# A stack of two transformer blocks on one core: the moving rows of the weight matmuls are read by turns from their two halves

## The chip, the cores and the metric

One NeuronCore of a Trainium2 chip runs the whole program. The metric is device time in microseconds (us) of one execution, lower is better. The core has a matrix engine (TensorE, PE in the profile), VectorE (DVE), ScalarE (ACT), GpSimd (POOL) and SyncE (SP, which only issues DMAs here). They run side by side and meet at semaphores. SBUF is the working memory (128 partitions), PSUM the memory into which TensorE accumulates, in eight banks of 512 f32 columns a partition.

## The reference, cut to what matters

256 rows of 1024 values (`x`) go through two stacks, each of two layers. Nearly all the work is products of these 256 rows with f32 weight matrices:

```python
def first_block(x, ...):
    for layer in range(2):
        h = h + _mixer(rmsnorm(h), w_in[layer], w_ret_o, w_sb_o, w_out)   # 1024 x 6656 weights, then 3 smaller ones
        h = h + (silu(hn @ Wg) * (hn @ Wu)) @ w_down                      # FF = 2816
    return rmsnorm(h)

def second_block(x, mem, ...):
    for layer in range(2):
        x = x + 0.5 * swiglu(rms_norm(x), ffn1_w_in, ffn1_w_out)
        x = x + mixer(rms_norm(x))            # attention kinds, even or odd layer
        x = x + memory_cross_attention(rms_norm(x), rms_norm(mem), w_q, w_kv, w_o)
        x = x + 0.5 * swiglu(rms_norm(x), ffn2_w_in, ffn2_w_out)
```

Between the big products stand small ones (retention, stick-breaking, forgetting, differential, banded and cross attention over at most 256 positions).

## The kernel before, in words

The 256 rows are two tiles of 128 (`T = 2`). An activation is turned (transposed) by TensorE, scaled, and kept as two fp32r tiles: a rounded value `hi` and the rest `lo`. A weight matrix is cut into units of 1024 columns a partition: two rows of 512 weights (`kk` = 0, 1) out of two blocks of 128 of the contraction. Each unit is loaded by a DMA into one of four buffers `RAW`, ScalarE rounds it into `WH` (L1066), and VectorE writes the rest `RAW - WH` into `WL` (L1287); `WH` and `WL` have five buffers each.

For each unit, row `kk` and tile `t`, TensorE runs three matmuls into the same PSUM bank: `hi*WH` (L785), `hi*WL` (L786), `lo*WH` (L787). The activation is the stationary operand (128x128, loaded by a weight load, PEld in the profile), and the row of 512 weights is the moving operand, which streams from SBUF. A "chunk" is a product with 512 output columns: over a contraction of 1024 it has 8 blocks x 2 tiles x 3 = 48 such matmuls, into a pair of banks (one for each `t`), and the pairs `M0, M1` and `M2, M3` take turns. When a chunk is done, ScalarE or VectorE empties both its banks: copies with a scale (L1071, L1074, L1080, L1099), SiLU of the gate columns 0..255 (L1095) and the product with the up columns 256..511 (L1350), the residual add (L1345), the merge of two branches (L1475, L1479). The small products and the transposes use four other banks, `AUX`.

The order of everything is fixed beforehand: `Plan` gives each step a due time, and each engine runs its steps sorted by it (`for_pe`, `for_act`, `for_dve`). The change does not touch the plan.

Of the kernel before, what the change touches and what calls it, by code (L numbers as in the profile page):

```python
# [11 lines left out]
ACT = mybir.ActivationFunctionType  # L12
# [145 lines left out]
class Tmp:  # L158
    def __init__(self, first):
        self.first, self.final, self.i = first, first, None  # L160


BANKED = ("turn", "tq", "ret_s", "ret_o", "st_z", "st_s", "st_o", "cu1", "cu2", "df_s", "pt", "df_o", "hg_s", "hg_o",
# [596 lines left out]
def tensor(e, k):  # L760
    p = k.p
# [3 lines left out]
    for s in p.for_pe:  # L765
# [3 lines left out]
        if s.kind == "mm":  # L769
            c = s.c  # L770
            h = s.u % NHL
# [8 lines left out]
            if s.at0 and c.use[s.t] > 1:  # L780
                e.wait_ge(k.m_out[c.banks[s.t]], c.use[s.t] - 1)
            out = p.M[c.banks[s.t]][:, 0:s.ncol]
            wh = p.WH[:, h, s.kk * s.ncol:(s.kk + 1) * s.ncol]
            wl = p.WL[:, h, s.kk * s.ncol:(s.kk + 1) * s.ncol]
            e.matmul(out, s.hi, wh, start=s.at0, stop=False)  # L785
            e.matmul(out, s.hi, wl, start=False, stop=False)  # L786
            i = e.matmul(out, s.lo, wh, start=False, stop=s.final)  # L787
            if s.unit_end:
                i.then_inc(k.w_used, 1)
        elif s.kind == "narrow":  # L790
            c = s.c
            h = s.u % NHL
# [3 lines left out]
            out = p.M[c.banks[0]][0:s.ncol, 0:256]  # L796
            for kt in range(s.nk):
                wh, wl = (x[:, h, kt * s.ncol:(kt + 1) * s.ncol] for x in (p.WH, p.WL))
# [3 lines left out]
                i = e.matmul(out, wh, xl, start=False, stop=kt == s.nk - 1)  # L802
# [26 lines left out]
        elif s.kind == "tq":  # L829
# [9 lines left out]
            x = p.TMP[s.x.i]  # L839
# [22 lines left out]
        elif s.kind == "ret_o":  # L862
            x = p.TMP[s.x.i]
# [8 lines left out]
        elif s.kind == "st_z":  # L872
# [6 lines left out]
            if s.mate is not None:  # L879
                z, x = s.mate, p.AUX[s.mate.bank]  # L880
# [18 lines left out]
        elif s.kind == "st_o":  # L899
# [13 lines left out]
            for x, v, out in zip(xs, s.v, outs):  # L913
                i = e.matmul(out[:, 128:256], v[:, 1, :], x[:, 128:256], start=False, stop=True)
            i.then_inc(k.aux_full[b], 1)
        elif s.kind == "cu1":
# [3 lines left out]
            x = p.TMP[s.x.i]  # L920
# [122 lines left out]
def scalar(e, k):  # L1043
# [5 lines left out]
    for s in p.for_act:  # L1049
# [3 lines left out]
        if s.kind in ("rope", "vals", "plainx", "ff", "hq", "rg"):  # L1053
            c = s.c
            e.wait_ge(k.w_used, c.done)
            if s.norm.n > r_have:
                r_have = s.norm.n
                e.wait_ge(k.r_made, r_have)
            banks = [p.M[x] for x in c.banks]
            r = [s.norm.r[:, t:t + 1] for t in range(T)]  # L1060
        if s.kind == "conv":
            i, h = s.u % NRAW, s.u % NHL
# [4 lines left out]
        elif s.kind in ("rope", "plainx"):  # L1067
            if s.kind == "rope" and s.n == 3:
                e.wait_ge(k.d_tabx, 16)
            for t in range(T):  # L1070
                e.activation(p.TMP[s.xs[t].i], banks[t][:, :], ACT.Copy, scale=r[t]).then_inc(k.m_out[c.banks[t]], 1)  # L1071
        elif s.kind == "vals":
            for t in range(T):
                e.activation(s.dst[t], banks[t][:, :], ACT.Copy, scale=r[t]).then_inc(k.m_out[c.banks[t]], 1)  # L1074
        elif s.kind == "gate":
            c = s.c
            e.wait_ge(k.w_used, c.done)
            e.wait_ge(k.rh_made, s.rh.n)
            for t in range(T):
                e.activation(s.dst[t], p.M[c.banks[t]][:, :], ACT.Copy, scale=s.rh.out[:, t:t + 1]).then_inc(k.m_out[c.banks[t]], 1)  # L1080
        elif s.kind == "rg":
            table = "s"
            for t in range(T):
                e.activation(s.silu[t], banks[t][:, :], ACT.Silu, scale=r[t]).then_inc(k.m_out[c.banks[t]], 1)
        elif s.kind == "tanh":
            table = "s"
            for q in s.gates:
# [4 lines left out]
        elif s.kind == "ff":  # L1092
            table = "s"
            for t in range(T):
                e.activation(s.silu[t], banks[t][:, 0:256], ACT.Silu, scale=r[t]).then_inc(k.silu_made, 1)  # L1095
        elif s.kind == "hq":
            for t in range(T):
                x = p.TMP[s.xs[t].i]
                e.activation(x, banks[t][:, :], ACT.Copy, scale=r[t]).then_inc(k.m_out[c.banks[t]], 1)  # L1099
                e.wait_ge(k.m_out[c.banks[t]], c.use[t])  # L1100
                if s.n > 1:
                    e.wait_ge(k.hq_sum, 2 * (s.n - 2) + t + 1)
                e.activation(p.AS[:, 2 * t:2 * t + 2, :].rearrange("p a c -> p (a c)"), x, ACT.Square).then_inc(k.hq_sq, 1)
# [161 lines left out]
def vector(e, k):  # L1265
# [4 lines left out]
    for s in p.for_dve:  # L1270
# [3 lines left out]
        if s.kind in ("ff", "ch", "res", "mer1", "mer2"):  # L1274
            c = s.c
            e.wait_ge(k.w_used, c.done)
            banks = [p.M[x] for x in c.banks]
        if s.kind in ("ff", "ch", "rh", "fin", "cu1"):
            if s.norm.n > r_have:
                r_have = s.norm.n  # L1280
# [40 lines left out]
        elif s.kind in ("st_o", "hg_o"):  # L1321
            e.wait_ge(k.hi_made, s.hi_n)
            e.tensor_tensor(s.lo, aux[:, 0:256], s.hi.bitcast(F32), ALU.subtract).then_inc(k.aux_out[b], 1)
        elif s.kind == "cx_o":
            e.wait_ge(k.hi_made, s.hi_n)
            e.tensor_tensor(s.lo, aux[:, :], s.hi.bitcast(F32), ALU.subtract).then_inc(k.aux_out[b], 1)
        elif s.kind == "gains":
            e.wait_ge(k.aux_out[b], s.use)
            if s.n == 3:
                for i in range(2):  # L1330
                    e.tensor_scalar(p.GT[:, 144 + i:145 + i], p.GT[:, 136 + 2 * i:137 + 2 * i], 0.125, None, ALU.mult)
                for i in range(4):
                    l, j = i // 2, i % 2
                    q = e.tensor_scalar(p.GT[:, 146 + i:147 + i], p.GT[:, 128 + 4 * l + j:129 + 4 * l + j], 0.0625, None, ALU.mult)
                q.then_inc(k.su_gain, 1)
        elif s.kind == "norm":
            e.wait_ge(k.sq_sum, 2 * s.sq.n)
            e.tensor_tensor(s.a, s.ss[:, 0:4:2], s.ss[:, 1:4:2], ALU.add).then_inc(k.dve_chain, 1)
            chain += 1
            e.wait_ge(k.dve_chain, chain)  # L1340
            e.tensor_scalar(s.v, s.a, 1.0 / D, EPS, ALU.mult, ALU.add).then_inc(k.ms_made, 1)
        elif s.kind == "res":
            for t in range(T):
                x = p.X[:, t, s.half * 512:(s.half + 1) * 512]
                e.scalar_tensor_tensor(out=x, in0=banks[t][:, :], scalar=s.scale, in1=x, op0=ALU.mult,  # L1345
                                       op1=ALU.add).then_inc(k.m_out[c.banks[t]], 1)
        elif s.kind == "ff":
            for t in range(T):
                e.wait_ge(k.silu_made, 2 * (s.n - 1) + t + 1)
                e.scalar_tensor_tensor(out=s.h[t], in0=banks[t][:, 256:512], scalar=r[t], in1=s.silu[t], op0=ALU.mult,  # L1350
                                       op1=ALU.mult).then_inc(k.m_out[c.banks[t]], 1)
        elif s.kind == "ret_s":
            if s.n == 1:
                e.wait_ge(k.d_dec, 16)
            e.wait_ge(k.aux_full[b], s.use)
            e.tensor_tensor(p.TMP[s.x.i][:, 0:384], aux[:, 0:384], p.DEC[:, s.h, :], ALU.mult).then_inc(k.aux_out[b], 1)
        elif s.kind == "ret_o":
            e.wait_ge(k.aux_out[b], s.use)
            e.bn_stats(s.st[:, 0:6], s.dst[:, 0, :])
            e.bn_stats(s.st[:, 6:12], s.dst[:, 1, :]).then_inc(k.dve_chain, 1)  # L1360
            chain += 1
            e.wait_ge(k.dve_chain, chain)
            e.bn_aggr(s.mv[:, 0:2], s.st[:, 0:6])
            e.bn_aggr(s.mv[:, 2:4], s.st[:, 6:12]).then_inc(k.dve_chain, 1)
            chain += 1
        elif s.kind == "ret_v":
            e.wait_ge(k.dve_chain, chain)
            e.tensor_scalar(s.v, s.mv[:, 1:16:2], 1.0, EPS, ALU.mult, ALU.add).then_inc(k.var_made, 1)
        elif s.kind in ("ret_n", "hn", "bo_n") and s.first_use:
            q = s.rs  # L1370
            e.wait_ge(k.rs_guess, q.n)
            e.tensor_tensor(q.a, q.y, q.y, ALU.mult).then_inc(k.dve_chain, 1)
            chain += 1
            e.wait_ge(k.dve_chain, chain)
            e.scalar_tensor_tensor(out=q.c, in0=q.a, scalar=-0.5, in1=q.v, op0=ALU.mult, op1=ALU.mult).then_inc(k.dve_chain, 1)
            chain += 1
            e.wait_ge(k.dve_chain, chain)
            e.scalar_tensor_tensor(out=q.out, in0=q.c, scalar=1.5, in1=q.y, op0=ALU.add, op1=ALU.mult).then_inc(k.dve_chain, 1)
            chain += 1
            e.wait_ge(k.dve_chain, chain)  # L1380
# [91 lines left out]
        elif s.kind == "mer1":  # L1472
            e.wait_ge(k.tanh_made, s.tanh.n)
            for t in range(T):
                e.scalar_tensor_tensor(out=p.TMP[s.xs[t].i], in0=s.g[t], scalar=1.0, in1=banks[t][:, :], op0=ALU.add,  # L1475
                                       op1=ALU.mult).then_inc(k.m_out[c.banks[t]], 1)
        elif s.kind == "mer2":
            for t in range(T):
                e.scalar_tensor_tensor(out=s.g[t], in0=s.g[t], scalar=1.0, in1=banks[t][:, :], op0=ALU.add,  # L1479
                                       op1=ALU.mult).then_inc(k.m_out[c.banks[t]], 1)  # L1480
            for t in range(T):
                x = p.TMP[s.xs[t].i]
# [64 lines left out]
            e.tensor_scalar(x[:, cut:end], x[:, cut:end], q.rc[:, 1:2], None, ALU.mult).then_inc(k.probs, 1)  # L1547
        elif s.kind == "ch":
            for t in range(T):
                x = p.TMP[s.xs[t].i]  # L1550
                e.wait_ge(k.m_out[s.cc.c.banks[t]], s.cc.c.use[t])
                e.scalar_tensor_tensor(out=x, in0=banks[t][:, :], scalar=r[t], in1=x, op0=ALU.mult, op1=ALU.mult).then_inc(k.m_out[c.banks[t]], 1)
        elif s.kind == "cv":
            if s.n == 1:
                e.wait_ge(k.zeroed, 2)
# [350 lines left out]
```

## Time and profile before

| what | us |
|---|---|
| median of 3 runs (lowest, highest) | 2069.71 (2069.34, 2070.16) |
| the profiled execution | 2067.88 |
| its span, first to last instruction | 2065.7 |
| TensorE busy | 2042.6 |
| VectorE busy | 1234.0 |
| ScalarE busy | 1111.7 |

Busy time says for how much of the span an engine had an instruction in it. Matmuls overlap in the pipeline, so the duration of one (0.39 us) is not what it costs: that is the distance from one start to the next, which the timeline and the chain show. The profiled execution lies 1.8 us below the median of the runs.

### The profile page before, as it was taken

Reading aid. Unit: us, or ns where it says so; the run is one execution under the profiler, and the core shown is the slowest. Engines: PE = TensorE matmul, PEld = TensorE weight load, DVE = VectorE, ACT = ScalarE, POOL = GpSimd, SP = SyncE. Lnnn points to the kernel's source line nnn. Section 1 sums busy time; section 2 is a strip of 40 time slices with the busy share of each in tenths; the row PEclk is TensorE's granted clock in tenths of the full one; section 3 lists DMA queues with packets and bytes.
Section 4 is the critical chain, followed back from the end, with each engine's and each line's share of the span. In section 5 each row is a group of like instructions: output and inputs, shape, how many; then the busy total and the mean of one; then the engine's idle time right before and its main releaser. Section 6 shows DMA issues by size and latency. Waiting matters only on the chain.

```text
span 2065.7 us, 25169 instructions
## 1 busy us (share of the span) xinstructions
PE 2042.6 (99%) x9627; PEld 1674.2 (81%) x9627; DVE 1234.0 (60%) x1721; ACT 1111.7 (54%) x1682; POOL 36.3 (2%) x60
## 2 busy tenths in 40 slices
PE   8999999999999999999999999999999999999999
PEld 7878888888778888888887888888888888788887
DVE  6576665565766655655567765655555566655553
ACT  6575544455755544644457665544444465655442
POOL 0000100000000000000000000000000000000000
PEclk9999999999999999999999999999999999999999
DMA  7545566555456665566554344565565553545653
GB/s 251 163 143 174 179 186 185 189 177 160 153 172 193 188 190 188 180 190 187 187 167 142 120 157 152 179 187 185 183 184 187 190 185 131 173 143 163 184 184 132
DMA packets 258214, 359.76 MB, mean 174 GB/s; under 512 B 16908, under 2 KB 152288, under 8 KB 258096
## 3 DMA queue, kind: packets, MB, share of 16 engines
q1 hardware_dynamic: 256016, 352.75, 54.2%
q0 software_dynamic: 2080, 5.41, 0.9%
q8 instruction: 77, 1.26, 0.2%
q14 instruction: 41, 0.34, 0.0%
HBM read 357.04 MB, written 1.06 MB: 173 GB/s over the span
## 4 chain that ended last, share of the span: by engine, by line
PE 94%; DVE 3%; ACT 2%; issue 1%; POOL 0%; DMA 0%; SPq 0%; DVEq 0%; ACTq 0%
PE M L785 28%; PE M L787 28%; PE M L786 28%; PE AUX L827 3%; DVE WL L1287 1%; PE AUX L841 1%; PE AUX L1039 1%; PE AUX L1017 1%; ACT WH L1066 1%; PE AUX L963 1%; PE AUX L978 0%; PE AUX L969 0%; DVE RET L1470 0%; DVE SM L1436 0%; PE AUX L1004 0%
## 5 line engine op out<-in xcount | busy, mean ns | idle before, releaser
L1287 DVE TENSOR_TENSOR WL<-RAW,WH 128x1024 fp32r<-128x1024 f32 x669 | 815.9, 1222 | 650.2 <-ACT WH L1066 647.4
L1066 ACT ACTIVATE WH<-RAW 128x1024 fp32r<-128x1024 f32 x669 | 706.5, 1058 | 660.6 <-PE M L787 654.5
L785 PE MATMUL M<-WH,Bh 128*128 128x512 f32 x1792 | 718.8, 401 | 2.3 <-DVE WL L1287 2.3
L787 PE MATMUL M<-WH,Bl 128*128 128x512 f32 x1792 | 700.3, 391 | 0.0
L786 PE MATMUL M<-WL,Bh 128*128 128x512 f32 x1792 | 699.4, 390 | 0.0
L787 PEld LDWEIGHTS M<-WH,Bl 128*128 128x128 f32 x1792 | 336.8, 188 | 72.5
L785 PEld LDWEIGHTS M<-WH,Bh 128*128 128x128 f32 x1792 | 337.2, 188 | 69.9 <-DVE WL L1287 2.7
L786 PEld LDWEIGHTS M<-WL,Bh 128*128 128x128 f32 x1792 | 337.7, 188 | 63.7
L1095 ACT ACTIVATE AS<-M,KEEP 128x256 f32<-128x256 f32 x132 | 55.3, 470 | 101.0 <-PE M L787 97.6
L785 PE MATMUL M<-WH,MTh 128*128 128x512 f32 x128 | 55.1, 430 | 0.0
L787 PE MATMUL M<-WH,MTl 128*128 128x512 f32 x128 | 50.5, 395 | 0.0
L786 PE MATMUL M<-WL,MTh 128*128 128x512 f32 x128 | 50.5, 395 | 0.0
L1345 DVE SCALAR_TENSOR_TENSOR X<-M,X 128x512 f32<-128x512 f32 x48 | 30.9, 685 | 20.9 <-PE M L787 20.8
L1116 ACT ACTIVATE Bh<-AUX,GTt 128x256 fp32r<-128x256 f32 x48 | 22.7, 474 | 29.0 <-PE AUX L827 29.0
L1312 DVE SCALAR_TENSOR_TENSOR Bl<-AUX,GTt,Bh 128x256 fp32r<-128x256 f32 x48 | 23.2, 483 | 25.3 <-ACT Bh L1117 25.3
L827 PEld LDWEIGHTS AUX<-CC,X 128*128 128x128 f32 x192 | 22.9, 144 | 15.3 <-issue 9.2
L785 PE MATMUL M<-WH,GA1h 128*128 128x512 f32 x88 | 34.5, 392 | 0.0
L785 PE MATMUL M<-WH,GA0h 128*128 128x512 f32 x88 | 34.5, 392 | 0.0
L785 PE MATMUL M<-WH,FA0h 128*128 128x512 f32 x88 | 34.5, 392 | 0.0
L785 PE MATMUL M<-WH,LA0h 128*128 128x512 f32 x88 | 34.5, 392 | 0.0
L785 PE MATMUL M<-WH,LA1h 128*128 128x512 f32 x88 | 34.3, 390 | 0.0
L785 PE MATMUL M<-WH,FA1h 128*128 128x512 f32 x88 | 34.3, 390 | 0.0
(415 smaller groups left out, 2503.2 us busy)
## 6 DMA issues: line engine op xcount, KB each, us to landing
RAW<-in_ffn_w_in SPq DMA_DIRECT2D x352, 256.0 KB, 3.3
RAW<-in_w_in SPq DMA_DIRECT2D x104, 512.0 KB, 3.6
RAW<-in_w_gate_up SPq DMA_DIRECT2D x176, 256.0 KB, 3.3
RAW<-in_ffn_w_out SPq DMA_DIRECT2D x88, 512.0 KB, 3.6
RAW<-in_w_down SPq DMA_DIRECT2D x44, 512.0 KB, 3.6
RAW<-in_x_w_kv SPq DMA_DIRECT2D x32, 512.0 KB, 3.6
RAW<-in_even_w_in SPq DMA_DIRECT2D x24, 512.0 KB, 3.8
RAW<-in_odd_w_in SPq DMA_DIRECT2D x24, 512.0 KB, 3.9
```

Of the source, the lines that this page charges most:

```text
L785: e.matmul(out, s.hi, wh, start=s.at0, stop=False)
L786: e.matmul(out, s.hi, wl, start=False, stop=False)
L787: i = e.matmul(out, s.lo, wh, start=False, stop=s.final)
L827: tr = e.transpose(aux[:, i * P:(i + 1) * P], x, ident)
L841: tr = e.transpose(aux[:, j * P:(j + 1) * P], x[:, j * P:(j + 1) * P], ident)
L963: e.matmul(out, s.q[:, q0:q0 + P], s.k[:, 0:kw], start=True, stop=False)
L1066: e.activation(p.WH[:, h, 0:s.size], p.RAW[:, i, 0:s.size], ACT.Copy).then_inc(k.w_hi, 1)
L1095: e.activation(s.silu[t], banks[t][:, 0:256], ACT.Silu, scale=r[t]).then_inc(k.silu_made, 1)
L1116: e.activation(s.hi[0], aux[:, 0:256], ACT.Copy, scale=s.gain[0])
L1287: e.tensor_tensor(p.WL[:, h, 0:s.size], p.RAW[:, s.u % NRAW, 0:s.size], hi.bitcast(F32), ALU.subtract).then_inc(k.w_lo, 1)
L1312: e.scalar_tensor_tensor(out=s.lo[0], in0=aux[:, 0:256], scalar=s.gain[0], in1=s.hi[0].bitcast(F32), op0=ALU.mult, op1=ALU.subtract)
L1345: e.scalar_tensor_tensor(out=x, in0=banks[t][:, :], scalar=s.scale, in1=x, op0=ALU.mult, op1=ALU.add).then_inc(k.m_out[c.banks[t]], 1)
```

## The change

The 512 weights of a row lie in SBUF as before. TensorE now reads them in the order 0, 256, 1, 257, 2, 258, ...: by turns from the two halves, which are 1024 bytes apart. The products so land in the bank in that order: bank column 2i holds output column i, and 2i+1 holds output column 256+i. Whoever empties a bank reads it with a step of two columns, first the even ones and then the odd ones, and writes (or reads with it) the two halves of an ordinary, unmixed destination. For the gated layers the even columns are the gate and the odd ones the up values. It is done by access patterns alone: no instruction is added, taken away or moved, and the matmuls' number, their stationary operands, the bank that they write and the waits stay. The narrow product (8 columns, L800 to L802) and the matmuls into `AUX` keep their order.

```diff
+def woven(x):
+    return x.rearrange("p (h i) -> p i h", h=2)
+
+def apart(bank):
+    return bank[:, :].rearrange("p (i h) -> p h i", h=2)
+
+def halves(x):
+    return x.rearrange("p (h i) -> p h i", h=2)
...
-            wh = p.WH[:, h, s.kk * s.ncol:(s.kk + 1) * s.ncol]
-            wl = p.WL[:, h, s.kk * s.ncol:(s.kk + 1) * s.ncol]
+            wh = woven(p.WH[:, h, s.kk * s.ncol:(s.kk + 1) * s.ncol])
+            wl = woven(p.WL[:, h, s.kk * s.ncol:(s.kk + 1) * s.ncol])
             e.matmul(out, s.hi, wh, start=s.at0, stop=False)
             e.matmul(out, s.hi, wl, start=False, stop=False)
             i = e.matmul(out, s.lo, wh, start=False, stop=s.final)
...
-                e.activation(p.TMP[s.xs[t].i], banks[t][:, :], ACT.Copy, scale=r[t]).then_inc(k.m_out[c.banks[t]], 1)
+                e.activation(halves(p.TMP[s.xs[t].i]), banks[t], ACT.Copy, scale=r[t]).then_inc(k.m_out[c.banks[t]], 1)
...
-                e.activation(s.silu[t], banks[t][:, 0:256], ACT.Silu, scale=r[t]).then_inc(k.silu_made, 1)
+                e.activation(s.silu[t], banks[t][:, 0, :], ACT.Silu, scale=r[t]).then_inc(k.silu_made, 1)
...
-                x = p.X[:, t, s.half * 512:(s.half + 1) * 512]
-                e.scalar_tensor_tensor(out=x, in0=banks[t][:, :], scalar=s.scale, in1=x, op0=ALU.mult,
+                x = halves(p.X[:, t, s.half * 512:(s.half + 1) * 512])
+                e.scalar_tensor_tensor(out=x, in0=banks[t], scalar=s.scale, in1=x, op0=ALU.mult,
                                        op1=ALU.add).then_inc(k.m_out[c.banks[t]], 1)
...
-                e.scalar_tensor_tensor(out=s.h[t], in0=banks[t][:, 256:512], scalar=r[t], in1=s.silu[t], op0=ALU.mult,
+                e.scalar_tensor_tensor(out=s.h[t], in0=banks[t][:, 1, :], scalar=r[t], in1=s.silu[t], op0=ALU.mult,
                                        op1=ALU.mult).then_inc(k.m_out[c.banks[t]], 1)
...
```

`banks` is now `[apart(p.M[x]) for x in c.banks]` on both engines; the other places that empty a bank are edited in the same way.

## Rows read from the trace of the kernel before

**Rows 1.** The page, part 1: busy us (share of the span) and instructions by engine.

```profile
span 2065.7 us, 25169 instructions
PE 2042.6 (99%) x9627; PEld 1674.2 (81%) x9627; DVE 1234.0 (60%) x1721; ACT 1111.7 (54%) x1682; POOL 36.3 (2%) x60
```

**Rows 2.** The page, part 4: the chain that ended last, by engine, by line.

```profile
PE 94%; DVE 3%; ACT 2%; issue 1%; POOL 0%; DMA 0%; SPq 0%; DVEq 0%; ACTq 0%
PE M L785 28%; PE M L787 28%; PE M L786 28%; PE AUX L827 3%; DVE WL L1287 1%; PE AUX L841 1%; PE AUX L1039 1%; PE AUX L1017 1%; ACT WH L1066 1%; PE AUX L963 1%; PE AUX L978 0%; PE AUX L969 0%; DVE RET L1470 0%; DVE SM L1436 0%; PE AUX L1004 0%
```

**Rows 3.** The page, part 5: groups, xcount, busy us, mean ns, idle before.

```profile
L1287 DVE TENSOR_TENSOR WL<-RAW,WH 128x1024 fp32r<-128x1024 f32 x669 | 815.9, 1222 | 650.2 <-ACT WH L1066 647.4
L1066 ACT ACTIVATE WH<-RAW 128x1024 fp32r<-128x1024 f32 x669 | 706.5, 1058 | 660.6 <-PE M L787 654.5
L785 PE MATMUL M<-WH,Bh 128*128 128x512 f32 x1792 | 718.8, 401 | 2.3 <-DVE WL L1287 2.3
L1095 ACT ACTIVATE AS<-M,KEEP 128x256 f32<-128x256 f32 x132 | 55.3, 470 | 101.0 <-PE M L787 97.6
L1345 DVE SCALAR_TENSOR_TENSOR X<-M,X 128x512 f32<-128x512 f32 x48 | 30.9, 685 | 20.9 <-PE M L787 20.8
```

**Rows 4.** Timeline of TensorE from 1000 us: start us, duration us, line, operands.

```profile
999.82 0.39 PE L785 MATMUL M<-WH,GA0h 128*128 128x512 f32 x1
1000.04 0.39 PE L786 MATMUL M<-WL,GA0h 128*128 128x512 f32 x1
...
1002.31 0.39 PE L787 MATMUL M<-WH,GA0l 128*128 128x512 f32 x1
```

**Rows 5.** The chain from 1223 us: start us, us on the chain, what.

```profile
1223.82 0.23 PE M L787
1224.05 1.73 PE AUX L1017 x8
1225.78 0.23 PE M L785
```

**Rows 6.** Timeline, 109 to 111 us: fp32r matmuls of 384 columns.

```profile
109.72 0.33 PE L895 MATMUL AUX<-SPL,UNR 128*128 128x384 f32 x1
109.89 0.34 PE L896 MATMUL AUX<-SPL,UNR 128*128 128x384 f32 x1
110.06 0.22 PE L897 MATMUL AUX<-SPL,UNR 128*128 128x128 f32 x1
```

**Rows 7.** The chain at the program's start.

```profile
10.51 0.43 PE M L786
10.94 0.43 PE M L787
...
12.64 0.43 PE M L785
13.07 0.41 PE M L786
13.48 0.24 PE M L787
```

**Rows 8.** Busy time by stretch: x is instructions; then granted clock, DMA share, GB/s.

```profile
1002.00:1016.00 14.00, 14.00 (x64) 11.58 (x63) 6.47 (x6) 5.58 (x6) 0.00 (x0) 1.00 0.55 190
1100.00:1270.00 170.00, 165.43 (x832) 133.31 (x831) 113.37 (x229) 106.74 (x237) 0.69 (x1) 1.00 0.39 131
1680.00:1870.00 190.00, 187.32 (x923) 153.28 (x922) 118.71 (x204) 109.62 (x201) 0.69 (x1) 1.00 0.45 147
```

**Rows 9.** Groups of DVE and ACT: the same work from PSUM and from SBUF.

```profile
L1502 DVE TENSOR_TENSOR AUX<-AUX,C 128x256 f32<-128x256 f32 x16 | 6.8, 426 | 4.3 <-PE AUX L969 3.3 <-PE AUX L945 1.0
L1450 DVE TENSOR_TENSOR DS<-DS,CC 128x256 f32<-128x256 f32 x16 | 6.8, 424 | 0.6
L1099 ACT ACTIVATE TMP<-M,KEEP 128x512 f32<-128x512 f32 x28 | 19.0, 679 | 12.4 <-PE M L787 12.4
```

**Rows 10.** The chain by time: an eviction on it, and the end of the program.

```profile
1099.40 0.70 ACT TMP L1099
...
1116.73 0.70 ACT TMP L1099
...
2061.86 0.69 DVE X L1345
2062.55 0.60 DVEq L1733
```

More of the change, by code:

```diff
@@ L1058, in scalar @@
                 e.wait_ge(k.r_made, r_have)
-            banks = [p.M[x] for x in c.banks]
+            banks = [apart(p.M[x]) for x in c.banks]
             r = [s.norm.r[:, t:t + 1] for t in range(T)]
@@ L1070, in scalar @@
             for t in range(T):
-                e.activation(p.TMP[s.xs[t].i], banks[t][:, :], ACT.Copy, scale=r[t]).then_inc(k.m_out[c.banks[t]], 1)
+                e.activation(halves(p.TMP[s.xs[t].i]), banks[t], ACT.Copy, scale=r[t]).then_inc(k.m_out[c.banks[t]], 1)
         elif s.kind == "vals":
             for t in range(T):
-                e.activation(s.dst[t], banks[t][:, :], ACT.Copy, scale=r[t]).then_inc(k.m_out[c.banks[t]], 1)
+                e.activation(halves(s.dst[t]), banks[t], ACT.Copy, scale=r[t]).then_inc(k.m_out[c.banks[t]], 1)
         elif s.kind == "gate":
@@ L1079, in scalar @@
             for t in range(T):
-                e.activation(s.dst[t], p.M[c.banks[t]][:, :], ACT.Copy, scale=s.rh.out[:, t:t + 1]).then_inc(k.m_out[c.banks[t]], 1)
+                e.activation(halves(s.dst[t]), apart(p.M[c.banks[t]]), ACT.Copy, scale=s.rh.out[:, t:t + 1]).then_inc(k.m_out[c.banks[t]], 1)
         elif s.kind == "rg":
@@ L1083, in scalar @@
             for t in range(T):
-                e.activation(s.silu[t], banks[t][:, :], ACT.Silu, scale=r[t]).then_inc(k.m_out[c.banks[t]], 1)
+                e.activation(halves(s.silu[t]), banks[t], ACT.Silu, scale=r[t]).then_inc(k.m_out[c.banks[t]], 1)
         elif s.kind == "tanh":
@@ L1098, in scalar @@
                 x = p.TMP[s.xs[t].i]
-                e.activation(x, banks[t][:, :], ACT.Copy, scale=r[t]).then_inc(k.m_out[c.banks[t]], 1)
+                e.activation(halves(x), banks[t], ACT.Copy, scale=r[t]).then_inc(k.m_out[c.banks[t]], 1)
                 e.wait_ge(k.m_out[c.banks[t]], c.use[t])
@@ L1276, in vector @@
             e.wait_ge(k.w_used, c.done)
-            banks = [p.M[x] for x in c.banks]
+            banks = [apart(p.M[x]) for x in c.banks]
         if s.kind in ("ff", "ch", "rh", "fin", "cu1"):
@@ L1474, in vector @@
             for t in range(T):
-                e.scalar_tensor_tensor(out=p.TMP[s.xs[t].i], in0=s.g[t], scalar=1.0, in1=banks[t][:, :], op0=ALU.add,
+                e.scalar_tensor_tensor(out=halves(p.TMP[s.xs[t].i]), in0=halves(s.g[t]), scalar=1.0, in1=banks[t], op0=ALU.add,
                                        op1=ALU.mult).then_inc(k.m_out[c.banks[t]], 1)
@@ L1478, in vector @@
             for t in range(T):
-                e.scalar_tensor_tensor(out=s.g[t], in0=s.g[t], scalar=1.0, in1=banks[t][:, :], op0=ALU.add,
+                e.scalar_tensor_tensor(out=halves(s.g[t]), in0=halves(s.g[t]), scalar=1.0, in1=banks[t], op0=ALU.add,
                                        op1=ALU.mult).then_inc(k.m_out[c.banks[t]], 1)
@@ L1549, in vector @@
             for t in range(T):
-                x = p.TMP[s.xs[t].i]
+                x = halves(p.TMP[s.xs[t].i])
                 e.wait_ge(k.m_out[s.cc.c.banks[t]], s.cc.c.use[t])
-                e.scalar_tensor_tensor(out=x, in0=banks[t][:, :], scalar=r[t], in1=x, op0=ALU.mult, op1=ALU.mult).then_inc(k.m_out[c.banks[t]], 1)
+                e.scalar_tensor_tensor(out=x, in0=banks[t], scalar=r[t], in1=x, op0=ALU.mult, op1=ALU.mult).then_inc(k.m_out[c.banks[t]], 1)
         elif s.kind == "cv":
```

## The prediction

> **What bounds the kernel now.** I read the busy shares first. TensorE is busy for 2042.6 of 2065.7 us, VectorE for 60% and ScalarE for 54% [rows 1]. Then the chain of waits: 94% of it is TensorE, and three lines, L785 to L787, hold 84% [rows 2]. These are the matmuls that the change touches. Their number comes from the weight units: 669 conversions [rows 3], of which one is the narrow unit; the other 668 feed 2 rows x 2 tiles x 3 products each, 668 x 12 = 8016 matmuls of 512 columns. That leaves one question: what does one of them cost. Its duration (0.39 us, 0.40 on the mean) is no answer, because the next starts before it ends. In the timeline of a quiet stretch the starts run from 999.82 to 1002.31 us over eleven steps (every line from L785 to L787 in turn, twelve rows, of which three are shown): 2.49 / 11 = 0.2264 us; the stretch after it has 64 matmuls in 14.00 us, 0.2188 with a few short ones for transposes in it [rows 4, 8]. I take 226.5 ns. 8016 x 0.2265 = 1816 us, 88% of the span. The other 250 us are matmuls into AUX and waits.
>
> 226.5 ns for 512 columns is 0.4424 ns a column. At 2.4 GHz, the upper of the two levels and the one that the granted clock of 1.00 stands for [rows 8], 512 columns would take 213.3 ns. So 13 ns in each matmul are something else, and three rows narrow down what:
> - Eight matmuls of 256 columns of plain f32 take 1.73 us on the chain, 216.3 ns each [rows 5]. They have the same weight loads of 128x128 before each of them, and spend as many clocks, since f32 runs at half the columns' pace. Their loss is only 3 ns. So neither the weight load nor the change from one matmul to the next explains 13 ns.
> - fp32r matmuls of 384 columns follow each other after 0.17 us [rows 6], 0.44 ns a column. The loss shrinks with the columns (160 ns would be without loss). It is a property of the stream.
> - At the program's start the same 512-column matmuls stand 0.43 us apart, from 10.51 to 13.07 us six of them, 426.7 ns [rows 7]: just 512 columns at 1.2 GHz, no loss. At half the pace the stream keeps up.
>
> So in-order reading of fp32r at one column a clock loses a sixteenth, and reading at half that pace loses nothing. That looks like the supply from SBUF, not the array.
>
> **The change, part by part.** *The moving operand.* The 8016 matmuls read the same bytes in another order. Each half of a row is then a stream of its own at half the pace, which is the pace at which the f32 stream and the slow-clock stream show no loss. No row of before has a moving operand with a step, so the price must be bounded from both sides:
> - lower end: no loss at all, 213.3 ns: 13.2 x 8016 = 106 us less;
> - nearest loss-free row: 216.3 ns [rows 5]: 10.2 x 8016 = 82 us less;
> - in between: nothing changes, 0;
> - upper end: the two columns that now come from one address region are fetched singly, and the stream falls to the pace of the f32 rows: 216.3 / 256 = 0.845 ns a column, 432.6 ns a matmul, 206 x 8016 = 1652 us more.
>
> I take 216.3 ns, because the loss of 13 ns has a place in the stream's order and its absence has a row, and because in these rows only the pace of a stream, not its bytes, decides over the loss. This is the step in which I am least sure.
>
> Of the 82 us not all arrive. In the two attention stretches, 1100 to 1270 and 1680 to 1870 us, TensorE runs 832 and 923 matmuls in 170 and 190 us, of which it is idle 4.6 and 2.7 [rows 8], and part of the chain there is on ACT and DVE; a faster matmul in them partly becomes a longer wait. They are 17% of the span; with half of their share given back some 7 us are lost. 82 - 7 = 75 us.
>
> *Who must keep up.* A unit's twelve matmuls fall from 2.72 to 2.60 us. Its conversion takes 1.06 us of ScalarE and 1.22 us of VectorE [rows 3], its load 512 KB, at 2.60 us 202 GB/s, against 190 GB/s at a DMA share of 0.55 [rows 8]: room in all three. ScalarE's wait before a conversion is on TensorE's L787 (654 us in all [rows 3]), so the buffers are filled ahead and shrink only by the difference. Nothing is late next.
>
> *The evictions.* Every read of a bank has a step of two columns. No row has such a step. From PSUM with two blocks and from SBUF the same work costs 426 and 424 ns [rows 9], so these engines take about a column a clock wherever it comes from, and I take the stepped read at nothing. The upper bound is a read at half the pace: a 512-column eviction costs 0.68 to 0.69 us [rows 3, 9], of which some 0.5 would come on top. Most evictions lie under the 48 matmuls (10.9 us) of the chunk in the other pair of banks, and cost nothing even then. On the chain are those before a transposition or an attention stage, such as L1099 at 1099.40 and 1116.73 us, and the last residual add [rows 10]; about twenty of them x 0.5 = 10 us. Below nothing I see no reason for a gain. Evictions of the gated layers take 256 columns in either order (L1095, 470 ns [rows 3]).
>
> *The sum.* On the profiled execution: 2067.9 - 75 = 1993 us. The median of the runs stood 1.8 us above it, so I predict 1995 us, with 1963 (no loss at all, everything arrives) to 2045 (a third of the gain, or the gain less slow evictions) for this case by itself.
>
> **The rivals.**
> 1. *The woven read runs at half pace.* Place: every one of the 8016 matmuls. For it speaks that f32 rows do run at 0.845 ns a column [rows 5], so there is a path that feeds one value every second clock; if the faster path lives from taking two neighbours in one fetch, weaving takes the neighbour away. Against it speaks that the loss of a sixteenth is no pattern of pairs. It decides from 227 ns up: each ns over it is 8 us. At 432.6 ns: 2068 + 1652 = 3720 us, less some 20 us of waits that TensorE's slower pace then covers: 3700. The Trainium skill ("Advanced Engine Details and Errata", Memory Cachelines) has a rule that gives this: SBUF is read in lines of 16 bytes, and at least two hits on a line are needed to absorb the latency of the memory. Four neighbours of a row share such a line and get their hits in order; woven, each read goes to the other line than the one before. No row of before can show it, since none steps.
> 2. *Slower by less.* The same mechanism with a smaller price (one more lost clock in sixteen, 13 ns x 8016 = 107 us, 2175), or an unchanged stream with the evictions at half pace (2080).
> 3. *Nothing changes.* The supply has lines of both halves open, the loss belongs to bytes and not to their order, and the stepped evictions are free: 2070. For it: the same bytes in the same time. Against: only that the slow-clock rows lose nothing for the same bytes, which a fixed rate explains as well.
>
> **How the numbers follow.** The stream without loss gets 0.44, half pace 0.34, slower by less 0.10, nothing 0.12. Cases of both signs hold most of the chance. The likeliest one's own range is 1963 to 2045; to leave out no more than 2 in 10 the range must reach the half pace, with its upper end at 3740. What a measurement of this kernel can tell from no change is about 0.2% (4 us): faster 0.44, same 0.12, slower 0.44.
>
> **What would show it.** In the timeline of a quiet stretch the distance of the starts of L785, L786 and L787 decides: 216 ns right, 227 the third rival, 430 the first. It must show in all stretches alike, the granted clock must stay at 1.00, and the start of the program, at 0.43 us, must not change in my case. In the half-pace case TensorE's share goes to nearly 100%, and VectorE's and ScalarE's fall to about a third. L1099 must stay at 0.68 us and L1345 at 0.685; at 1.2 the stepped read is not free. What would make the prediction wrong is any price of the alternation itself: it is the only term that is not read from a row of the same kind.

## The result, and the profile after

The changed kernel takes 1982.51 us (median of 4 runs, 1981.84 to 1983.48) against 2069.53 us (4 runs, one more than in the table ahead of the prediction, 2069.14 to 2070.16): a ratio of 0.958, with a 95% interval of 0.9563 to 0.9596. The profiled execution took 1981.93 us with a span of 1979.7, so 86.0 us less of span than before.

The first lines of the page of the changed kernel, and its chain by engine (what answers to [rows 1, 2]):

```profile
span 1979.7 us, 25169 instructions
PE 1947.5 (98%) x9627; PEld 1684.7 (85%) x9627; DVE 1233.1 (62%) x1721; ACT 1109.0 (56%) x1682; POOL 36.3 (2%) x60
...
PE 90%; DVE 5%; ACT 3%; issue 1%; POOL 1%; DMA 0%; SPq 0%; DVEq 0%; ACTq 0%
```

The same instructions on every engine, the same busy time on VectorE and ScalarE to within 3 us, and 95 us less on TensorE. The chain still is TensorE's, though ACT and DVE have gone from 5% to 8% of it. Lines have moved by 16: L801 to L803 are the former L785 to L787.

TensorE's timeline in the stretch of the first gated product of the second stack (what answers to [rows 4]: start, duration, line, operands):

```profile
959.30 0.38 PE L803 MATMUL M<-WH,GA0l 128*128 128x512 f32 x1
959.51 0.38 PE L801 MATMUL M<-WH,GA0h 128*128 128x512 f32 x1
...
961.89 0.38 PE L803 MATMUL M<-WH,GA0l 128*128 128x512 f32 x1
```

Twelve steps in 2.59 us: 0.2158 us from start to start, where [rows 4] had 0.2264. Of the 8015 distances after a matmul of 512 columns, taken from the starts in both traces, the undisturbed ones (up to 229 ns before, up to 220 after) have a mean of 226.7 ns before (6128 of them) and 215.8 ns after (7626 of them). 512 columns at 2.4 GHz are 213.3, so 2.5 ns of loss are left of 13.4.

Where the 86.0 us came from, with the same distances summed:

| part | us |
|---|---|
| 8015 distances, each at the undisturbed mean, 226.7 to 215.8 ns | -87 |
| distances of 230 to 260 ns (nearly all of them up to 236), 1508 before and none after: their excess | -10 |
| longer distances (a wait before the next matmul, or the first steps after matmuls into AUX): excess 52.1 before, 61.6 after | +9.5 |
| distances after matmuls into AUX, 179.6 before, 181.1 after | +1.5 |
| sum | -86 |

Taking the two traces matmul by matmul (both have the same 9627 in the same order), the last two rows of the table can be placed: of their 11 us, 4.7 were lost in the two attention stretches of [rows 8], the rest elsewhere, at other places where TensorE waits for ScalarE or VectorE before it can go on.

The program's start, at TensorE's slower pace (what answers to [rows 7]; timeline):

```profile
10.79 0.63 PE L803 MATMUL M<-WH,Bl 128*128 128x512 f32 x1
11.22 0.63 PE L801 MATMUL M<-WH,Bh 128*128 128x512 f32 x1
...
13.35 0.63 PE L803 MATMUL M<-WH,Bl 128*128 128x512 f32 x1
```

Six steps in 2.56 us, 426.7 ns, as before: at 1.2 GHz there was no loss to win back. That this is the lower level is read from the rows themselves, from 426.7 ns for 512 columns and from weight loads of 0.33 us, where they take 0.19 later; the profile's granted clock prints 1.00 here too, and its first entry lies behind this stretch. The evictions, which now read their banks with a step of two columns (what answers to [rows 3]):

```profile
L1111 ACT ACTIVATE AS<-M,KEEP 128x256 f32<-128x256 f32 x132 | 55.4, 471 | 93.1 <-PE M L803 89.4
L1361 DVE SCALAR_TENSOR_TENSOR X<-M,X 128x512 f32<-128x512 f32 x48 | 30.9, 686 | 17.2 <-PE M L803 17.2
```

471 and 686 ns, where they took 470 and 685. The copies that the prediction named, L1099 and now L1115, took 679 ns both times.

### The profile page after: what moved, and what is told of

The parts are those of the page before. It is cut to its first block, busy times and chain, and to the rows that moved or that the text cites. A ratio compares the mean times of both kernels' runs of the same rounds, so it can differ in the third digit from the quotient of the medians.

```text
span 1979.7 us, 25169 instructions
## 1 busy us (share of the span) xinstructions
PE 1947.5 (98%) x9627; PEld 1684.7 (85%) x9627; DVE 1233.1 (62%) x1721; ACT 1109.0 (56%) x1682; POOL 36.3 (2%) x60
## 3 DMA queue, kind: packets, MB, share of 16 engines
q0 software_dynamic: 2080, 5.41, 0.9%
## 4 chain that ended last, share of the span: by engine, by line
PE 90%; DVE 5%; ACT 3%; issue 1%; POOL 1%; DMA 0%; SPq 0%; DVEq 0%; ACTq 0%
PE M L801 27%; PE M L803 27%; PE M L802 27%; PE AUX L843 3%; DVE WL L1303 2%; ACT WH L1082 1%; PE AUX L857 1%; PE AUX L1055 1%; PE AUX L1033 1%; PE AUX L979 1%; DVE SM L1452 1%; ACT TMP L1115 0%; DVE TMP L1409 0%; PE AUX L994 0%; PE AUX L985 0%
## 5 line engine op out<-in xcount | busy, mean ns | idle before, releaser
L1303 DVE TENSOR_TENSOR WL<-RAW,WH 128x1024 fp32r<-128x1024 f32 x669 | 815.7, 1222 | 583.1 <-ACT WH L1082 580.1
L1082 ACT ACTIVATE WH<-RAW 128x1024 fp32r<-128x1024 f32 x669 | 704.8, 1055 | 591.5 <-PE M L803 583.0
L801 PE MATMUL M<-WH,Bh 128*128 128x512 f32 x1792 | 698.7, 390 | 2.3 <-DVE WL L1303 2.3
L802 PE MATMUL M<-WL,Bh 128*128 128x512 f32 x1792 | 680.0, 379 | 0.0
L803 PE MATMUL M<-WH,Bl 128*128 128x512 f32 x1792 | 679.9, 379 | 0.0
L801 PEld LDWEIGHTS M<-WH,Bh 128*128 128x128 f32 x1792 | 339.4, 189 | 49.2 <-DVE WL L1303 2.8
L803 PEld LDWEIGHTS M<-WH,Bl 128*128 128x128 f32 x1792 | 339.2, 189 | 48.2
L802 PEld LDWEIGHTS M<-WL,Bh 128*128 128x128 f32 x1792 | 339.8, 190 | 42.6
L801 PE MATMUL M<-WH,MTh 128*128 128x512 f32 x128 | 53.0, 414 | 0.0
L802 PE MATMUL M<-WL,MTh 128*128 128x512 f32 x128 | 48.5, 379 | 0.0
L803 PE MATMUL M<-WH,MTl 128*128 128x512 f32 x128 | 48.5, 379 | 0.0
L843 PE MATMUL AUX<-CC,X 128*128 128x128 f32 x192 | 30.6, 285 | 5.3 <-DMA X<-in_x 2.3
L857 PE MATMUL AUX<-CC,TMP 128*128 128x128 f32 x192 | 29.2, 275 | 4.7 <-DVE TMP L1409 4.7
L801 PE MATMUL M<-WH,FA0h 128*128 128x512 f32 x88 | 33.6, 382 | 0.0
L801 PE MATMUL M<-WH,GA0h 128*128 128x512 f32 x88 | 33.6, 382 | 0.0
L801 PE MATMUL M<-WH,LA0h 128*128 128x512 f32 x88 | 33.6, 382 | 0.0
L801 PE MATMUL M<-WH,GA1h 128*128 128x512 f32 x88 | 33.6, 382 | 0.0
```

The lines of the kernel that those rows point to most:

```text
L843: tr = e.transpose(aux[:, i * P:(i + 1) * P], x, ident)
L857: tr = e.transpose(aux[:, j * P:(j + 1) * P], x[:, j * P:(j + 1) * P], ident)
L1082: e.activation(p.WH[:, h, 0:s.size], p.RAW[:, i, 0:s.size], ACT.Copy).then_inc(k.w_hi, 1)
L1303: e.tensor_tensor(p.WL[:, h, 0:s.size], p.RAW[:, s.u % NRAW, 0:s.size], hi.bitcast(F32), ALU.subtract).then_inc(k.w_lo, 1)
```

## The experiments

All but e4 and e11 change one thing in the kernel before: the order in which the 512 columns of a row are streamed. Their evictions stay as they were, so the columns of each product lie in a mixed order; the amount of work and every instruction's size are the same. Each of e1 to e10 was executed once; they move by much more than the 2.3 us by which 13 executions of the kernel before differ (2068.28 to 2070.53), or else by less. The edit is in each case

```diff
+def in_order(x):
+    return x.rearrange(...)
...
-            wh = p.WH[:, h, s.kk * s.ncol:(s.kk + 1) * s.ncol]
-            wl = p.WL[:, h, s.kk * s.ncol:(s.kk + 1) * s.ncol]
+            wh = in_order(p.WH[:, h, s.kk * s.ncol:(s.kk + 1) * s.ncol])
+            wl = in_order(p.WL[:, h, s.kk * s.ncol:(s.kk + 1) * s.ncol])
```

with the pattern given at each run. "A group" below is 16 bytes, four f32 columns that start at a multiple of four. Each fence shows TensorE's timeline of that kernel in the same product as above.

**e1: how far apart must the two places be?** `"p (b h i) -> p b i h", h=2, i=4`.

> Both rows of weights are read by turns from two neighbouring groups of four columns: 0, 4, 1, 5, 2, 6, 3, 7, 8, 12, ... (16 bytes apart, where the changed kernel has 1024). The evictions are those of the kernel before, so the columns of each product stay in the mixed order; no work is left out. Theory A (any alternation between two places relieves the supply of the stream): 216 ns from matmul to matmul, about 1980 us. Theory B (the two places must lie far apart, in different parts of the memory): the loss of a sixteenth stays, 227 ns, about 2069 us, or more. Half pace (the rival that fell) would be 430 ns.

1983.02 us, beside 2069.15 for the kernel before.

```profile
958.88 0.38 PE L791 MATMUL M<-WH,GA0l 128*128 128x512 f32 x1
...
961.47 0.38 PE L791 MATMUL M<-WH,GA0l 128*128 128x512 f32 x1
```

Twelve steps in 2.59 us, 215.8 ns. Theory A: two neighbouring groups do as well as two that lie 1024 bytes apart. This run has the evictions of before and the time of the changed kernel, so it also says that the stepped evictions cost nothing that shows.

**e2: a step instead of a turn.** `"p (i h) -> p h i", h=2`.

> The row is read with a step of two columns, first the 256 even columns, then the odd ones; evictions as before, so the columns stay mixed. No alternation, but two columns of every 16 bytes instead of four. If the loss belongs to the bytes passed over (one lost clock for each 64 bytes), it doubles: 240 ns a matmul, some 107 us more, 2175 us. If it belongs to neighbouring columns read one after the other in pairs, it goes: 216 ns, about 1980 us. If it belongs to the number of columns whatever their order, 227 ns.

3836.81 us. None of the three: a matmul now costs twice as much.

```profile
1877.40 0.63 PE L789 MATMUL M<-WH,GA0h 128*128 128x512 f32 x1
...
1882.81 0.63 PE L789 MATMUL M<-WH,GA0h 128*128 128x512 f32 x1
```

Twelve steps in 5.41 us, 451 ns. The half pace of my first rival exists, but for another order than I feared. It is also no matter of the clock. At this kernel's start (timeline), where 512 columns at 1.2 GHz would take 426.7 ns,

```profile
10.80 0.64 PE L790 MATMUL M<-WL,Bh 128*128 128x512 f32 x1
...
13.53 0.63 PE L790 MATMUL M<-WL,Bh 128*128 128x512 f32 x1
```

six steps take 2.73 us, 455 ns: almost the same as at the upper level. That the clock was the lower one there shows in the weight loads, 0.31 us each against 0.21 later:

```profile
11.26 0.31 PEld L789 LDWEIGHTS M<-WH,Bh 128*128 128x128 f32 x1 [0.15 <-issue]
...
1877.40 0.21 PEld L790 LDWEIGHTS M<-WL,GA0h 128*128 128x128 f32 x1 [0.24 <-issue]
```

So what limits this order reads as a time and not as a number of TensorE's clocks; e9 and e10 below say the same (460 and 453 ns at the start, 461 and 452 later). With two columns of each group in a pass, a row needs 256 changes of group: 451 / 256 = 1.76 ns each. In order it needs 128 changes in 226.7 ns: 1.77 ns each. That gave the idea of a fixed time for each change of group.

**e3: turns of four columns.** `"p (h i j) -> p i h j", h=2, j=4`.

> By turns four columns from the first half and four from the second (16 bytes from each); evictions as before, columns mixed. If it is enough that the stream changes its place every few columns: 216 ns a matmul and about 1980 us. If the turn must come with every single column: 227 ns and about 2069 us.

2232.38 us.

```profile
1083.34 0.41 PE L791 MATMUL M<-WH,GA0l 128*128 128x512 f32 x1
...
1084.84 0.41 PE L791 MATMUL M<-WH,GA0l 128*128 128x512 f32 x1
```

Six steps in 1.50 us, 250 ns, neither of the two forecasts. Turns with whole groups don't help; they are worse than reading in order by 23 ns.

**e4: is it the weight load?** The kernel before with one line edited:

```diff
-            e.matmul(out, s.hi, wl, start=False, stop=False)
+            e.matmul(out[0:64], s.hi[:, 0:64], wl, start=False, stop=False)
```

> The kernel before, in-order reading; only the second product (activation hi times WL) has a stationary operand of 64 instead of 128 columns, so half of the rows of each tile lack this small correction. Its weight load, which lies beside the stream of the matmul before it, is half as long. My theory (the loss is the stream's own): from the first product to the second 227 ns as for the others, time unchanged but for the odd ns. The rival (each weight load takes its reads out of the stream's supply): the distance from the first to the second product falls to about 220 ns, the two others stay at 227, and the time falls by 2672 x 6.5 ns = 17 us.

2085.54 us, 16 us slower.

```profile
1010.73 0.39 PE L785 MATMUL M<-WH,GA0h 128*128 128x512 f32 x1
1010.96 0.40 PE L786 MATMUL M<-WL,GA0h 128*64 128x512 f32 x1
1011.19 0.39 PE L787 MATMUL M<-WH,GA0l 128*128 128x512 f32 x1
...
1013.48 0.39 PE L785 MATMUL M<-WH,GA0h 128*128 128x512 f32 x1
```

The weight load before the second product, of the kernel before and of this run:

```profile
L786 PEld LDWEIGHTS M<-WL,Bh 128*128 128x128 f32 x1792 | 337.7, 188 | 63.7
L786 PEld LDWEIGHTS M<-WL,Bh 128*64 128x64 f32 x1792 | 241.4, 135 | 67.6
```

It has half the columns and takes 135 ns where it took 188, so it is shorter, but not by half. The distance from the first product to the second nevertheless has a median of 228 ns (0.23 in these rows), and the forecast of 220 ns is not met. The rival of the weight loads falls: a lighter load gave nothing back. The 16 us come mostly from the two other distances, whose median has risen from 227 to 231 ns; why, this run doesn't say.

**e5: out of order, but group by group.** `"p (b h i) -> p b i h", h=2, i=2`.

> The order 0, 2, 1, 3, 4, 6, 5, 7, ...: a turn with every column, but all four columns of each 16 bytes are read before the next 16 are touched. Evictions as in the kernel before, columns mixed. Line theory (the stream pays for each change from one group of 16 bytes to the next, about 1.77 ns each, and a turn helps only because two groups are open at once): one group at a time as in order, so 227 ns and about 2069 us. Turn theory (it is enough that no two neighbouring columns follow each other): 216 ns and about 1982 us.

2068.21 us, beside 2070.10 for the kernel before.

```profile
1001.35 0.39 PE L791 MATMUL M<-WH,GA0l 128*128 128x512 f32 x1
...
1004.07 0.39 PE L791 MATMUL M<-WH,GA0l 128*128 128x512 f32 x1
```

Twelve steps in 2.72 us, 226.7 ns. That neighbours don't follow each other is worth nothing; groups count.

**e6: turns of two columns.** `"p (h i j) -> p i h j", h=2, j=2`.

> By turns two columns from the first half and two from the second: 0, 1, 256, 257, 2, 3, 258, 259, ...; columns stay mixed. Groups of 16 bytes stay open over two visits here. If two groups are open at once and the turn only has to come before a group is used up: 216 ns, about 1982 us. If every return to a group costs like a new one (256 visits): about 450 ns as in the run with a step of two columns, 3830 us. Between them (about 250 ns, as with turns of four): the turn must come with every column.

2871.21 us.

```profile
1400.74 0.51 PE L791 MATMUL M<-WH,GA0l 128*128 128x512 f32 x1
...
1404.68 0.51 PE L791 MATMUL M<-WH,GA0l 128*128 128x512 f32 x1
```

Twelve steps in 3.94 us, 328 ns, and 333 in many others (331 on the mean): between the numbers that I had written down.

**e7: turns of one column, with a step of two.** `"p (h i j) -> p j i h", h=2, j=2`.

> By turns from the two halves, but with a step of two columns in each: 0, 256, 2, 258, ..., then 1, 257, 3, 259, ...; columns stay mixed. Every group of 16 bytes is visited twice for two columns each, 256 groups' fetches a row as in the run with a step of two, but two of them open at a time. If the two open groups are fetched beside each other: 216 to 240 ns. If the fetches follow each other at 1.77 ns: 451 ns and about 3830 us.

2068.73 us.

```profile
1001.81 0.39 PE L791 MATMUL M<-WH,GA0l 128*128 128x512 f32 x1
...
1004.53 0.39 PE L791 MATMUL M<-WH,GA0l 128*128 128x512 f32 x1
```

226.7 ns, just the in-order number, though this order changes groups with every single column and comes to each group twice. That is what turned the idea of e2 into a theory of two readers: the columns at even places of the stream (the first, third, fifth, ...) are fetched by one reader, those at odd places by another, side by side, and each reader needs 1.76 to 1.77 ns for every change to a new group. The array itself needs 213 ns a row, and the slower of the two sets the pace. Then what counts is how many columns *a reader* takes out of a group in a row:

| order | first columns | of one group in a row, for each reader | changes for each reader | at 1.77 ns | measured, ns |
|---|---|---|---|---|---|
| in order | 0 1 2 3 4 | 2 | 128 | 227 | 226.7 |
| e5 | 0 2 1 3 4 | 2 | 128 | 227 | 226.7 |
| e7 | 0 256 2 258 | 2 | 128 | 227 | 226.7 |
| e2 | 0 2 4 6 | 1 | 256 | 453 | 451 |
| halves (the change) | 0 256 1 257 | 4 | 64 | 113, so the array's 213 | 215.8 |
| e1 | 0 4 1 5 | 4 | 64 | 113, so the array's 213 | 215.8 |

By this table the loss of a sixteenth in the kernel before is no loss at every sixteenth column: it is 128 changes at 1.77 ns, 227, which happen to lie just above the array's 213.

**e8: four places.** `"p (h i) -> p i h", h=4`.

> By turns from the four quarters: 0, 128, 256, 384, 1, 129, ...; columns stay mixed. Four groups of 16 bytes are open at once. If the supply keeps four or more open: 216 ns, about 1982 us. If it keeps two: each column is a new fetch, 512 of them, 900 ns if they follow each other and 450 ns if two run beside each other; 3800 us or more.

2443.11 us.

```profile
1189.02 0.44 PE L789 MATMUL M<-WH,GA0h 128*128 128x512 f32 x1
...
1192.30 0.44 PE L789 MATMUL M<-WH,GA0h 128*128 128x512 f32 x1
```

Twelve steps in 3.28 us, 273 ns; over the whole program these distances lie between 270 and 287 ns, with a mean of 277. None of the forecasts (216, 450, 900) is met. Each reader here goes to and fro between two quarters with every column.

**e9 and e10: the theory put to the test.** A step of four, `"p (i h) -> p h i", h=4`, and a step of four with turns between the halves, `"p (h i j) -> p j i h", h=2, j=4`. For two readers both are 256 changes each; a single reader, or a turn that makes changes cheap, gives quite other times.

> The row is read with a step of four columns in four passes: 0, 4, 8, ..., then 1, 5, 9, ...; columns stay mixed. Two-reader theory (the columns at even places of the stream and those at odd places are fetched by two readers side by side, and each needs about 1.76 ns for every change to another 16 bytes, whatever the clock): each reader changes with each of its 256 columns, as with a step of two, so 451 ns a matmul again and about 3840 us. One-reader theory (1.76 ns for each change of the whole stream): 512 changes, 902 ns and about 7400 us.

3914.60 us.

```profile
1914.98 0.66 PE L791 MATMUL M<-WH,GA0l 128*128 128x512 f32 x1
...
1920.51 0.66 PE L791 MATMUL M<-WH,GA0l 128*128 128x512 f32 x1
```

Twelve steps in 5.53 us, 461 ns: 1.80 ns a change, 2% over the forecast, and half of what one reader would need.

> By turns from the two halves with a step of four columns: 0, 256, 4, 260, ...; columns stay mixed. Two-reader theory: each reader walks through one half and changes its 16 bytes with each column, 256 changes, 451 ns and about 3840 us. If it is the turn between the halves that makes changes cheap (with a step of two it stood at 227 ns): 227 to 340 ns, 2070 to 3000 us.

3838.10 us.

```profile
1878.70 0.63 PE L789 MATMUL M<-WH,GA0h 128*128 128x512 f32 x1
...
1884.12 0.63 PE L789 MATMUL M<-WH,GA0h 128*128 128x512 f32 x1
```

Twelve steps in 5.42 us, 452 ns. The turn between the halves is no help by itself: with one column from each group it is as slow as plain steps, with two as slow as reading in order (e7), and only with four is it fast.

**e11: the evictions alone.** The changed kernel, with the weights read in order:

```diff
-            wh = woven(p.WH[:, h, s.kk * s.ncol:(s.kk + 1) * s.ncol])
-            wl = woven(p.WL[:, h, s.kk * s.ncol:(s.kk + 1) * s.ncol])
+            wh = p.WH[:, h, s.kk * s.ncol:(s.kk + 1) * s.ncol]
+            wl = p.WL[:, h, s.kk * s.ncol:(s.kk + 1) * s.ncol]
```

> The other half of the change alone: the weights are read in order, as in the kernel before, and the banks are read with a step of two columns as in the changed one, so the columns of each product are mixed. If stepped reads of a bank are free for ScalarE and VectorE: 2069.5 us, within 0.1%; L1095 at 470 ns and L1345 at 685 ns. If they cost half the pace: 1.2 us for an eviction of 512 columns and about 2080 us.

2069.01 us against 2069.49 us, ratio 0.9999 (0.9990 to 1.0009). From its page:

```profile
L1111 ACT ACTIVATE AS<-M,KEEP 128x256 f32<-128x256 f32 x132 | 55.4, 471 | 101.0 <-PE M L803 97.6
L1361 DVE SCALAR_TENSOR_TENSOR X<-M,X 128x512 f32<-128x512 f32 x48 | 30.9, 686 | 20.8 <-PE M L803 20.7
```

The stepped reads of the banks are free within 2 us, and with e1 it is settled from both sides: the whole gain, within this, is the order of the moving rows.

**What stays open.** The theory in its simple form (a reader keeps one group and pays 1.77 ns for each change) fits the eight orders in which a reader goes on to new groups, or stays within one. In three orders each reader leaves for a place far away and it does not fit: e3 (two columns, then 1024 bytes away) should be 227 ns and is 250; e6 and e8 (to and fro with each column, coming back to the same group) should be 451 and are 331 and 277 on the mean. So coming back to a group just left costs less than a new one: 277 / 256 = 1.08 ns a change in e8, 1.29 in e6. If a new group costs 1.77 ns there too, an estimate for a return follows from both: in e8 each reader has 64 new groups and 192 returns, (277 - 64 x 1.77) / 192 = 0.85 ns, in e6 128 of each, (331 - 128 x 1.77) / 128 = 0.82 ns. That the two agree speaks for a reader that keeps the group it left last within reach. e3 has no returns, only jumps of 1024 bytes to new groups, and fits this no better: 250 / 128 = 1.95 ns against 1.77. Whether the two places get in each other's way stays open: the same turns at a short distance, which would tell it, were not tried.

That there are two readers is a reading of these times, the simplest that gives e2, e7, e9 and e10 together, and no run looks at them directly. A rival gives the same numbers for all eight orders: one reader that fetches the columns in pairs, each with the one behind it, and pays 1.77 ns for a pair that leaves the groups of the pair before it. In every order tried here both columns of a pair go to new groups together, so no run tells the two apart.

## Why the prediction was right

It forecast 1995 us with 1963 to 2045 for the likeliest case by itself, and 1982.5 was measured. The path and the place of the loss were right; the reason given for the price of the new order was right only in part. Point by point:

- **What bounds the kernel, and where 13 ns go.** Right. The 8016 matmuls at 226.5 ns were measured again at 226.7, and nothing but their distance had to fall. The argument from rows that the loss belongs to the stream was borne out: e4 speaks against the weight load (one of 135 ns in place of 188 gave nothing back), the start of the program kept its 426.7 ns, and orders alone move the time between 216 and 461 ns.
- **The term of the sum.** I took the price of a loss-free row, 216.3 ns, from plain f32 matmuls [rows 5], and the woven stream costs 215.8: 82 us forecast, 87 measured. The reason that I gave for it, "each half of a row is then a stream of its own at half the pace, which is the pace at which the f32 stream and the slow-clock stream show no loss", holds in its first half. Its second half is too little: the half pace by itself does not do it. e7 and e10 also give each half a stream of its own at half the pace, and they run at 227 and 452 ns. What relieves a reader is the number of columns that it takes from one group, four where it took two. So there is luck in this term: by the same reason I would have forecast 216 ns for e7, and its 227 would have refuted me; the order that was chosen is one of those for which it comes out.
- **What the attention stretches give back.** I sized 7 us in the two attention stretches; 4.7 were lost there, and another 6 at waits elsewhere, which the sum left out, 11 us in all. In the chain, the cross attention's stretch from the reduction L1436 (now L1452) to the first scores L1017 (now L1033) took 1224.05 - 1104.20 = 119.85 us before [rows 5, and the row below] and 1174.84 - 1058.07 = 116.77 after, 2.6% less where the whole program has 4.2%. The row of before, then those of after:

```profile
1104.20 1.20 DVE SM L1436 x2
```

```profile
1058.07 1.20 DVE SM L1452 x2
...
1174.84 1.73 PE AUX L1033 x8
```

- **The term that was missing.** 1508 distances of 230 to 260 ns, nearly all of them up to 236, stood in the trace of before, and I had left them out of the sum. All are gone after, another 10 us. They remain in e5, e7 and e11, the orders at 227 ns (1488 to 1525 of them), and there is none in e1. That reads like an extra delay that shows when the supply has no slack and is covered when it has; what makes it, no run shows. The 10 us with 5 from the first term, less 4 for the waits, are 11 of the 12.5 us between 1995 and 1982.5; the rest is the 1.8 us that I added for the difference between the runs and the profiled execution, which was 0.6 after the change.
- **Nothing late next, evictions free.** Right. Conversions took 1055 and 1222 ns a unit, where they took 1058 and 1222, and TensorE's waits on L1303 before L801 stayed at 2.3 us; the evictions are settled by e11.
- **The rivals.** The half pace got a chance of 0.34 and did not come. Its mechanism, that a read which has no neighbour in its group beside it halves the pace, is real, and e2, e9 and e10 have it; the mistake would have been to count neighbours along the stream instead of those that one reader sees. The rule of the Trainium skill behind it ("Advanced Engine Details and Errata", Memory Cachelines), two hits on a line of 16 bytes to absorb the latency, agrees with the runs in the size of the group, read by the table: with groups of 8 bytes e5 would have been as fast as e1, and with groups of 32 bytes e9 would have taken twice the time of e2, where they take 461 and 451 ns. It does not agree in the number: the order in e2 takes two columns of every 16 bytes and runs at half pace, in-order reading takes four and still loses a sixteenth. If there are two readers, each has its two hits in order (226.7 ns) and only one in e2 (451); but two are still not enough for the 213 of 2.4 GHz, and four are (215.8). Nor is a line lost when the stream touches another one in between, as the woven order does with every column. The measurement decides. The other two rivals (slower by less, nothing changes) needed a smaller price or none, and fell with 215.8 ns.

## What to carry to other kernels

Whoever has a kernel that TensorE bounds and that streams fp32r rows of 512 columns should look at the distance of the matmuls' starts: if it is 227 ns where 216 would do, an access pattern alone, without a single new instruction, gives back 4.8% of each. Let the moving row be read by turns, column by column, from two places, so that each place is itself read in unbroken order; 16 bytes apart does as well as 1024. With two halves, whoever empties the bank can undo the mixing at no cost by a step of two columns; for the places 16 bytes apart the undoing was not run. A moving row with a step of two or of four columns (a de-interleaved view) is the thing to avoid: it doubled the matmul, and turns of two or four columns or from four places cost 10% to 46% of one.

## What the runs showed of the hardware that I had not expected

- In eight orders the time of an fp32r row fits a fixed time for each change of 16-byte group, about 1.77 ns, at either of TensorE's levels: 451 ns a row at the upper and 455 at the lower one in e2. Three other orders (e3, e6, e8) need another price.
- The times fit only if this is counted separately for the columns at even and at odd places of the stream, or for pairs of them (e7 at 227 ns against e2 at 451, with the same 256 visits to groups in all; e9 at 461, half of what 512 changes in a row would take).
- VectorE and ScalarE read a PSUM bank with a step of two f32 columns at full pace (686 and 471 ns, unchanged).
- The scatter of 230 to 260 ns between matmuls, which looked like the price of something next to TensorE, disappears with the same change (1508 to none).
